# Modulation products beside the 24 gates, and matrix loads behind the second fetch

## The reference

```python
mod = silu_c @ w_ada[l] + b_ada[l]              # 6 vectors of 1024, for both streams
h = modulate(rmsnorm(x, g_mix[l]), sh1, sc1)
p = h @ w_in[l]
x = x + gt1 * latent_mixer(p, ...)              # attention, conv, then merge_branches
h2 = modulate(rmsnorm(x, g_ffn[l]), sh2, sc2)
x = x + gt2 * expert_choice_ffn(h2, w_router[l], w_e_gate[l], w_e_up[l], w_e_down[l])

def merge_branches(o_a, o_b, o_c, gate_logits, w_branch, w_out):
    g_a, g_b, g_c = jnp.split(jax.nn.sigmoid(gate_logits), 3, axis=-1)
    merged = g_a * (o_a @ w_branch[0]) + g_b * (o_b @ w_branch[1]) + g_c * (o_c @ w_branch[2])
    return merged @ w_out

def expert_choice_ffn(h, w_router, w_g, w_u, w_d):   # each of 16 experts takes its best n / 8 rows
    aff = jax.nn.softmax(h @ w_router, axis=1)
    gate, idx = lax.top_k(aff, cap)
    xs = h[bi, idx]
    y = (silu(xs @ w_g) * (xs @ w_u)) @ w_d
    return zeros.at[bi, idx].add(y * gate)
```

## Time and profile before

| | us |
|---|---|
| median of three runs | 3527.5 (3526.8 to 3530.91) |
| the profiled execution, device time | 3523.05 |
| its span | 3521.2 |
| TensorE busy | 3275.4 (93%) |
| VectorE busy | 1241.1 (35%) |
| ScalarE busy | 1004.2 (29%) |
| DMA moved | 617.00 MB, mean 175 GB/s |

### The profile page before, as it was taken

The page is one execution under the profiler, slowest core; times in us unless marked ns, Lnnn a source line. Parts: engine busy times, 40 slices in busy tenths (PEclk is TensorE's granted clock), DMA queues, the critical chain, the costliest instruction groups (busy, mean ns, idle before and its releaser), DMA issues.

```text
span 3521.2 us, 48003 instructions
## 1 busy us (share of the span) xinstructions
PE 3275.4 (93%) x21250; PEld 2200.7 (62%) x21250; DVE 1241.1 (35%) x1821; ACT 1004.2 (29%) x1571; POOL 225.4 (6%) x142
## 2 busy tenths in 40 slices
PE   6999999999699999989999996988879999989998
PEld 4787667888334343467768882332328766858887
DVE  3335642233401011145563333111125444353333
ACT  3623541122210001037353222000022354342223
POOL 0100000121100000001000220000002010120000
PEclk9999999999799999999999998999999999989999
DMA  7540014222899999833102329999983121323331
GB/s 216 148 146 25 1 49 121 66 61 60 322 397 398 389 351 389 313 63 82 43 1 71 97 91 366 421 421 421 422 329 85 36 59 37 96 60 97 101 96 66
DMA packets 385614, 617.00 MB, mean 175 GB/s; under 512 B 99234, under 2 KB 288896, under 8 KB 360704
## 3 DMA queue, kind: packets, MB, share of 16 engines
q1 hardware_dynamic: 378064, 596.50, 48.0%
q0 software_dynamic: 4384, 15.73, 1.3%
q10 hardware_dynamic: 2960, 1.71, 0.2%
HBM read 606.54 MB, written 7.34 MB: 174 GB/s over the span
## 4 chain that ended last, share of the span: by engine, by line
PE 81%; DMA 10%; DVE 4%; ACT 3%; issue 1%; POOL 0%; ACTq 0%; SPq 0%; DVEq 0%
PE ps L592 33%; PE ps L1843 6%; PE ps L2227 5%; PE ps L1083 4%; DMA ring<-in_w_e_up 4%; PE ps L1172 3%; PE ps L1846 3%; DMA ring<-in_w_e_down 3%; PE ps L1879 3%; PE ps L1133 3%; PE ps L644 3%; PE ps L1347 3%; PE ps L1838 2%; PE ps L613 2%; PE ps L1884 2%; PE ps L1875 2%
## 5 line engine op out<-in xcount | busy, mean ns | idle before, releaser
L592 PE MATMUL ps<-xh,wh 128*128 128x512 f32 x1912 | 638.1, 372 | 19.2 <-DVE xl L2073 9.3
L592 PE MATMUL ps<-xl,wh 128*128 128x512 f32 x1912 | 630.4, 368 | 0.0
L592 PE MATMUL ps<-xh,wl 128*128 128x512 f32 x1912 | 630.1, 367 | 0.0
L565 DVE TENSOR_TENSOR wl<-ring,wh 128x1024 fp32r<-128x1024 f32 (+1 forms) x259 | 332.1, 1283 | 443.6 <-ACT wh L556 441.8
L592 PEld LDWEIGHTS ps<-xh,wh 128*128 128x128 f32 x1912 | 330.4, 189 | 101.3 <-issue 23.8
L556 ACT ACTIVATE wh<-ring 128x1024 fp32r<-128x1024 f32 (+1 forms) x259 | 272.0, 1051 | 421.2 <-PE ps L592 161.8
L592 PEld LDWEIGHTS ps<-xh,wl 128*128 128x128 f32 x1912 | 330.4, 189 | 61.2
L592 PEld LDWEIGHTS ps<-xl,wh 128*128 128x128 f32 x1912 | 330.1, 189 | 58.6 <-issue 0.5
L1843 PE MATMUL ps<-ring,arena 128*32 128x512 f32 x1344 | 176.6, 597 | 0.9 <-ACT arena L1592 0.9
L1838 PE MATMUL ps<-ring,arena 128*64 128x512 f32 x704 | 161.7, 602 | 11.7 <-DMA ring<-in_w_e_up 7.1
L1094 DVE TENSOR_REDUCE sm<-ps 128x2 f32<-128x1536 f32 (+3 forms) x96 | 142.3, 1482 | 41.8 <-PE ps L1083 41.4
(11 more groups left out here) (277 smaller groups left out, 4440.0 us busy)
## 6 DMA issues: line engine op xcount, KB each, us to landing
ring<-in_w_e_gate SPq DMA_DIRECT2D x87, 1024.0 KB, 19.5
ring<-in_w_e_up SPq DMA_DIRECT2D x85, 1024.0 KB, 19.9
ring<-in_w_e_down SPq DMA_DIRECT2D x85, 1024.0 KB, 20.9
ring<-in_w_in SPq DMA_DIRECT2D x112, 512.0 KB, 4.1
ring<-in_w_ada SPq DMA_DIRECT2D x96, 512.0 KB, 5.0
arena<-in_w_e_up SPq DMA_DIRECT2D x43, 1024.0 KB, 18.7
arena<-in_w_e_down SPq DMA_DIRECT2D x43, 1024.0 KB, 20.0
arena<-in_w_e_gate SPq DMA_DIRECT2D x41, 1024.0 KB, 21.0
```

The costliest lines, as they stand in the source:

```text
L565: e.tensor_tensor(in_heads(X, u, m.WL[:, o:o + many]), heads_of(X, u, halves.aps[s], many), in_heads(X, u, m.WH[:, o:o + many].bitcast(F32 ...
L592: i = e.matmul(ps[0:M, a:b], w[:, k, 0:M], h[:, k, a:b], start=k == 0 and p == 0, stop=k == 7 and p == 2)
```

## The change

Two things. First, layer 1's modulation: products 64 to 95 move from behind the gates, where they were spread over the end of the merge and the choice, to gates 8 to 23, two for each gate (and 48 to 63 stand in twos behind each gate too, behind the branch products where there are any). Their loads move in SP's list accordingly. `act_mod(4)` stands at t = 15 and `act_mod(5)` at t = 23; `pe_modt` and `dve_mod` of pair 4 ahead of gate 16, of pair 5 ahead of output product 2. Second, `dve_gates` and those expert loads that waited for the index product wait for the second fetch of the layer as well (`s_g[1]` at 16 in layer 0, and at 144 in layer 1, of which 128 are layer 0's).

```diff
@@ mixer_weights
-                    if t < 8:
-                        mods(48 + 2 * t)
                     if d % 2:
                         X.split(("b", br, d), 256, branch(l, br, d - 1, 256))
                         if t < 23:
                             gate(t + 1)
-                    if t < 8:
-                        mods(49 + 2 * t)
+                    mods(48 + 2 * t, 49 + 2 * t)
             for d in range(KD):
                 X.split(("o", d), 128, column(I["w_out"][l], 128 * d))
-            mods(*range(64, 96))
@@ pe_merge
-                    if l == 0 and t == 8:
-                        pe_modt(e, 3)
+                    if l == 0 and t in (8, 16):
+                        pe_modt(e, 2 + t // 8)
                     pe_linear3(e, X, ("g", br, d), 128, T, (X.key, "g", t), g_sg.at(X.key, t))
-                    if l == 0 and t < 8:
-                        pe_mod(e, 48 + 2 * t)
...
-                    if l == 0 and t < 8:
+                    if l == 0:
+                        pe_mod(e, 48 + 2 * t)
                         pe_mod(e, 49 + 2 * t)
             for d in range(KD):
+                if l == 0 and d == 2:
+                    pe_modt(e, 5)
...
-            if l == 0:
-                for m in range(64, 68):
-                    pe_mod(e, m)
@@ act_merge
-                    if l == 0 and t == 7:
-                        act_mod(e, 3)
+                    if l == 0 and t % 8 == 7:
+                        act_mod(e, 3 + t // 8)
                     if d % 2:
                         act_high(e, X, X.unit["b", br, d] + 1)
@@ dve_merge
-                    if l == 0 and t == 8:
-                        dve_mod(e, 3)
+                    if l == 0 and t in (8, 16):
+                        dve_mod(e, 2 + t // 8)
...
             for d in range(KD):
+                if l == 0 and d == 2:
+                    dve_mod(e, 5)
@@ pe_choice, act_choice, dve_choice
-            mods(*range(68, 80))
...
-            mods(*range(80, 88))
...
-            if l == 0:
-                pe_modt(e, 4)
...
-            mods(*range(88, 96))
-            if l == 0:
-                pe_modt(e, 5)
...
-            if l == 0:
-                act_mod(e, 4)
...
-            if l == 0:
-                act_mod(e, 5)
...
-            if l == 0:
-                dve_mod(e, 4)
...
-                dve_mod(e, 5)
@@ dve_gates
             e.wait_ge(*r_dve.at(st, "pick"))
+            e.wait_ge(s_g[1], 144 if l else 16)
```

More of the change, by code:

```diff
@@ L372, in build @@
         A1v = A1[:, :].rearrange("p (l m k w) -> p l m k w", l=2, m=2, w=2)
-        MR = lambda pair: tmp[:, 3840:4352] if pair < 4 else AR(21504, 512)
+        MR = tmp[:, 3840:4352]
         mcol = lambda l, which, k, w: modv[:, l, 8 * which + k, w:w + 1]
@@ L674, in act_mod @@
                 e.wait_ge(*p_modt.at("mod", pair - 1))
-            e.activation(MR(pair), bank.of["mod", pair][:, 0:512], ACT.Copy).then_inc(*c_mod.up("mod", pair))
+            e.activation(MR, bank.of["mod", pair][:, 0:512], ACT.Copy).then_inc(*c_mod.up("mod", pair))
         def pe_modt(e, pair):
@@ L682, in pe_modt @@
             for c in range(4):
-                i = e.transpose(ps[:, 128 * c:128 * c + 128], MR(pair)[:, 128 * c:128 * c + 128], ident)
+                i = e.transpose(ps[:, 128 * c:128 * c + 128], MR[:, 128 * c:128 * c + 128], ident)
             i.then_inc(*p_modt.up("mod", pair))
@@ L1484, in pe_choice @@
             m = ME[l]
-            def mods(*tiles):
-                for m in tiles if l == 0 else ():
-                    pe_mod(e, m)
-            mods(*range(68, 80))
             ps, when = bank.take((st, "lgp"), r_act.at(st, "lgp"))
```

## The result

The changed kernel takes 3544.97 us (median of six, 3542.96 to 3547.57), the kernel before 3527.15 (median of six beside it, 3524.08 to 3530.91): a ratio of 1.0050, 95% interval 1.0039 to 1.0061. It is slower by 17.8 us. The profiled execution's span is 3544.8 us, where before has 3521.2. These two executions lie 23.6 us apart, more than the medians: 3.3 us of that arose ahead of the first gate, and 3.3 behind the second block's expert matrices, where nothing was changed. Both stretches vary among all the profiled executions (first gate at 493.64 to 498.39 us; 928.0 to 931.5 us behind the last matrix in the chain, experiment 2 left out). One of the eleven executions in experiment 2 took 10366.98 us at a mean granted clock of 0.30, and the ratio there is formed without it.

A forecast was written before the change was run, and what follows sets the result against it. TensorE was taken to bound the merge and the first block's experts, matrix transfers the second block's. Merge +36.9, choice -19.0 and second block -1.0 gave +16.9 us on 3527.5: 3544.4 us, range 3532 to 3551.

The forecast's parts named there:

- Products beside the gates: Merge, gates 8 to 23: products cost 2.90 us per pair of gates; eight new pairs +23.2, four old ones -0.6.
- The two small boundaries: Merge, gates 8 and 16: gate 8's 2.97 us gap and 1.70 restart recur at gate 16, +4.7 us.
- The boundary ahead of the output products: End of merge: ScalarE's copy at t = 23 delays the first output product; 9.7 us gap, +9.9 with restart.
- The merge as a whole: All gates and output products: the added products, gaps and transposes sum to +36.9 us.
- the -0.7 for gates 8 and 16: Merge: these gates come behind a wait and transposes instead of products, so run at the fast pace, -0.7 us.
- The choice: First block, last square to first expert product: without products there, index product 15.4 us sooner, -19.0 with the fetch.
- The fetch: First block's choice: with expert matrices waiting it takes 4.7 us instead of 8.31, -3.6.
- First block's experts, no cost: Four matrices wait for the first fetch but arrive with the first product; TensorE bounds the stage: 0.
- The step that failed: Second block: without two matrices the rows land 3.0 us sooner; net -1.0 us, bounds -3.5 and +2.5.
- The boundaries don't gap: Rival, merge: ScalarE's copies of pairs 4 and 5 finish in time, both gaps go; 3529.8 us, chance 0.14.
- The queued matrices cost in the second block: Rival: two deferred matrices leave the DMA idle, +2.5 us instead of -1.0; 3547.9 us, chance 0.10.
- Late rows: Rival, first block's choice: early expert matrices delay the rows' landing in h2d, +5 us; 3549.4 us, chance 0.05.

The follow-up runs named there:

- experiment 2: The kernel before with only the two waits for the second fetch added, products not moved: 3528.65 us, ratio 1.0004.
- experiment 6: Against experiment 4: four products behind the branch products of each odd gate, none behind the even one: 3521.70 us, ratio 0.9983.
- experiment 8: Against experiment 4: without the wait of `dve_gates`, so VectorE writes GX, GC and zeros at once: 3528.12 us, ratio 1.0002.
- experiment 4: The changed kernel with ScalarE's copies of the sums of pairs 3, 4 and 5 put later: 3525.34 us, ratio 0.9999.
- experiment 5: Against experiment 4: pair 5's copy back at t = 23, ahead of the copies to XH: 3538.42 us, ratio 1.0035.
- experiment 7: Against experiment 4: products 90 to 95 put between the sums of squares and the router product: 3524.01 us, ratio 0.9992.
- experiment 1: The changed kernel without both waits for the second fetch, products moved alone: 3546.93 us, ratio 1.0058.
- experiment 3: The changed kernel with both waits in the first block (layer 0) only: 3541.09 us, ratio 1.0042.
- `best`: Against experiment 4: waits in the first block only, products in fours, products 92 to 95 and pair 5's copy in the choice: 3517.09 us, ratio 0.9973.
- experiment 9: Against experiment 4: waits in the first block only; three second-block matrices wait until the rows are in `h2d`: 3523.17 us, ratio 0.9989.

## Why the prediction was right

The medians differ by 17.8 us and 16.9 were forecast; nearly every term of the sum can be found in the chain of after.

- **Products beside the gates.** Forecast 28.02 for a pair of gates (25.12 + 2.90), measured 27.83. The bulk of the miss is that a branch product directly behind a gate takes 8.48, not 8.66: in the new order no product stands ahead of it. Eight new pairs cost 21.7 us (23.2 forecast), the four old ones gained 1.3 (0.6). The 8.68 behind products, on which the term rests, holds in all pairs; experiment 6 showed that most of it is the position directly behind products, and that the 8.33 without them can also be 8.48.
- **The two small boundaries.** The row at gate 8 carried over to gate 16 without a change: 2.97 us again, and 1.7 to 1.9 for the restart. Forecast 4.7, measured 4.8.
- **The boundary ahead of the output products.** A gap of 9.74, where 9.7 was worked out, and 1.8 us more for the first two outputs (18.50 for 16.70), where 1.7 was. Together +10.0 for +9.9. The transposes of pair 5 took 0.44, for 0.4.
- **The output products behind these transposes.** Not in the sum: 50.90 us for six, where before six took 50.1 (six eighths of 66.80), +0.8, at the slower pace of experiment 6.
- **The merge as a whole** went from 386.66 to 422.55 us (gate 0 to the end of the last output product), +35.9 for +36.9. The terms as measured, with the -0.7 for gates 8 and 16, make 34.9, and 35.7 with the output products' 0.8.
- **The choice** gained 20.5 us, from the last square to the first expert product, for 19.0. The router's copy came 3.8 us sooner (4.4 forecast), the fold product 11.4 (12.0), the index product 16.3 (15.4), the fetch took 4.2 less (3.6). What was not in my sum: the fold product itself, 1.50 us instead of 2.69. Before, TensorE had been waiting for matrices of w_ada, and the fold ran at the lower level; after, it came straight from the router product, at the upper one. The window of before over its fold product has a granted clock of 0.50, the one of after 1.00 (before first):

```profile
910.30:913.00 2.70, 2.70 (x13) 2.70 (x14) 0.01 (x1) 0.00 (x0) 0.00 (x0) 0.50 1.02 419
...
938.00:940.00 2.00, 1.48 (x12) 1.41 (x12) 0.35 (x2) 0.00 (x0) 0.00 (x0) 1.00 0.00 0
```

- **The fetch.** I took 4.7 us, between 4.3 alone and 5.04 beside two matrices; it was 4.07 with nothing beside it. By the Trainium skill (DMA: Bandwidth & Descriptors, section "Queues, rings and completion order") and that page's 2.0 us + bytes / 436 GB/s I had set an estimate of 2.9 alone and 3.8 beside a queue against that, and so 1 us for the waiting. The traces have 4.07 alone and 8.94 beside four matrices with VectorE writing GX; the measurement decides, and it gives 4.9, of which some 0.5 are VectorE's (experiment 8).
- **First block's experts, no cost.** From their first product to 598 us behind it nothing differs: 950.80 to 1548.94 before, 969.43 to 1567.69 after. The four matrices that wait arrive beside work, as the earlier trace rows said.

**The step that failed** is the small one on the second block, -1.0 forecast, +1.6 measured. Its working said that the two deferred matrices stand between the rows and the end of the transfer, so that the rows land 3.0 us sooner. They landed 0.6 sooner, by the chain of after against the earlier trace rows:

```profile
2156.91 15.69 DMA h2d<-rows
2172.60 0.26 issue
2172.86 4.50 DMA taken<-h2d,aff
```

The windows of after around that landing show what the sum of bytes left out:

```profile
2169.50:2170.00 0.50, 0.00 (x0) 0.00 (x0) 0.00 (x0) 0.00 (x0) 0.00 (x0) 0.50 0.46 189
2170.00:2170.50 0.50, 0.00 (x0) 0.00 (x0) 0.00 (x0) 0.00 (x0) 0.00 (x0) 0.50 0.12 49
...
2171.50:2172.00 0.50, 0.00 (x0) 0.00 (x0) 0.00 (x0) 0.00 (x0) 0.00 (x0) 0.50 0.04 16
```

The bulk is in at 2170, but the rows count as landed at 2172.60, behind a tail of 2.6 us in which the DMA is busy for 0.12 and less. Before, with the two matrices queued behind the rows, the share stays at 0.95 and more until they count as landed at 2154.52. Bytes divided by the rate put the rows' end ahead of such a tail, at 2151.5; with the 2.6 us on top it is 2154.1, close to the 2154.52 of before. So the 3.0 us that I gave to the last two matrices were mostly the tail's. Over all kernels the rows take 14.3 to 15.9 us from the last issue with the wait in the second block (seven kernels: after, experiments 2 and 4 to 8) and 14.3 to 17.1 without it (four: before, 1, 3 and `best`): no gain can be told there. The Trainium skill (DMA: Bandwidth & Descriptors, section "Anatomy of one DMA — SWDGE (gpsimd) path") puts most of a fixed 2 us of a transfer into waiting for the last byte to be confirmed. The size fits; but the window still has some bytes moving, so whether the tail is slow last writes or their confirmation stays open.

What the deferral costs then shows in the time from the second block's router product to its last matrix. With the wait in the second block it is 472.5 to 474.9 us in six kernels (after and experiments 4 to 8), without it 470.6 to 472.4 in four (before, experiments 1, 3 and `best`). The means of these two groups lie 2.0 us apart, for a bound of +2.5 in the prediction; the medians of after and experiment 3 say 2.8, within their uncertainty. Experiment 2 is left out here, since its chain goes through another matrix. From the router product to the end of the span, which takes it in, the seven kernels with the wait have 1401.0 to 1404.7 us (it has 1404.7), the four without 1399.7 to 1401.2. I call the sign shown and the size open within 1 to 3 us.

**The rivals.** "The boundaries don't gap" is refuted by the chain (2.97, 2.97, 9.74), and experiment 4 measured its price by taking the cause away: the merge falls by 18.7, where the prediction's terms give 4.7 for each of the two small boundaries (the one at gate 8 was there before) and 9.9 for the large one, 19.3. Experiment 5 splits it: 7.5 for the two, where the terms give 9.4, and 11.2 for the third, where they give 9.9; the two errors cancel in part. "The queued matrices cost in the second block" did come true, by 1 to 3 us, on top of the forecast and not in its place. "Late rows" did not: the index product's results were ready at 962.25 and the fetch started with that, without a wait for `h2d`.

So the total came within 1 us partly by luck, by terms that cancel: the merge 1.0 cheaper than forecast, the choice 1.5 better, the second block 2.6 worse.

## What to carry to other kernels

Work moved beside a busy engine's main loop costs its own time plus whatever its consumer's copy holds up in another engine's queue; here 32 products cost some 20 us and three copies standing a few places too early cost another 19 (5 of them before the change already), and that was free to avoid. Put such a copy behind the work that the next product waits for, and look for the places where TensorE waits for another engine anyway (the norm ahead of the router product took six products for 0.7 us). The wait that keeps bulk transfers away from a short, urgent one took 5.1 us out of the first block's choice, but only once nothing else was still queued (experiments 1 and 2); in the second block, where the transfers set the stage's end, it cost 1 to 3. Look at both before you add one.

## What the runs showed of the hardware

- A fetch by indirect DMA of the rows of one expert round took 4.07 to 4.45 us alone in the first block. Issued together with matrices of 1 MB on SP's queue or just behind them it took 8.31 to 9.11: beside eleven, of which seven were issued ahead of it, 8.31 (before), beside seven 8.47 (experiment 2), beside five 9.11 (experiment 9), beside four 8.94 (experiment 1). So from four up the number made no plain difference. With two matrices in the second block it depended on how far ahead the first was issued: 3.7 and 3.8 us ahead, 6.17 and 6.57 (experiments 3 and 1); 5.8 and 6.4 us ahead, 5.04 and 4.71 (before and `best`).
- The rows written to DRAM counted as landed at 2172.60 in the kernel after, 2.6 us after the DMA's share had fallen to 0.12 and less; it was 0.91 over 2168 to 2170.
- A gate of 48 matmuls takes 8.68 us directly behind modulation products (32 columns of weights). Away from them gates and output products run at 8.33 to 8.35 us or at 8.48, and keep that over many blocks: eight output products took 66.80 us (before), 66.82 (experiment 7) and 68.09 (`best`). The traces show that, not its cause.
- A gap of 2.97 us on TensorE with four transposes in it was followed by the lower clock level (a granted clock of 0.60 over 3.6 us) and cost 1.7 to 1.9 us besides itself, against gates of 8.33; behind gaps of 1.50 and 1.51 us (before, and `best`) the granted clock was 1.00. Behind the gaps of 9.7 us the first two output products took 1.8 and 2.4 us more (after, and experiment 5).
- VectorE's writes of GX hold up GpSimd's issue of a fetch: 3.71 us instead of 0.94 (experiment 8 against 4).
